# Expert stage: gathering the tokens of four experts at once, token pieces stationary and 256 pick columns moving, no turning of tokens

## The chip, the cores and the metric

One Trainium2 chip, one of its cores. The metric is the device time of one launch in microseconds (us); the median of three runs of the kernel before is 2372.9 us (2370.32 to 2373.47).

## The reference, cut to what matters

The reference is two transformer blocks on 512 tokens of width 1024. The change touches only the last part of the second block, a mixture of 32 experts. Each token is routed to two experts of one group; an expert is a gated feed-forward of width 256:

```
y[e] = (silu(h @ w_gate[e]) * (h @ w_up[e])) @ w_down[e]     # [1024x256], [1024x256], [256x1024]
x    = x + gt2 * sum over the token's two experts of weight * y[e]
out  = rms_norm(x) * g_final
```

The kernel computes an expert only for tokens that picked it: at most 64 of them (64 "slots") in a round. With these inputs one round is enough, so that the stage is 16 pairs of experts, each run once. All is float32; the weights of a pair are six tensors of 1 MB.

## The kernel before, in words

**What runs where.** The expert stage is written out by hand for five engines, which meet at semaphores. SyncE (line 630, helper `expert_load`) issues six loads of 1 MB for each pair of experts: two gate, two up, two down. All but pair 1 use the same six buffers `EXPERT_W`; pair 1 has six of its own (`SECOND_W`). The weights of pairs 0 and 1 are loaded ahead, while the router still works. A load into a buffer waits until the matmuls that read it are done: the gate loads of the next pair wait for the first half of `gu_done`, the up loads for the second, the down loads for `down_made`. Pairs 2, 3, 4 and so on are thus each loaded while the pair ahead of them is computed, part by part.

**One pair on TensorE** (`expert_pair`). (1) Gate and up, line 1366: for each of the two parts and each of the 8 pieces of the model width, one float32 matmul for each expert of the pair, with 64 columns of tokens stationary and 256 weight columns moving; the two experts use different halves of the array. 64 records in the trace. (2) Two `gather` calls for the *next* pair, line 1339: `PICKS` (a 0/1 matrix that says which token goes to which slot, 128 tokens x 128 slots, one for each of four blocks of tokens) is stationary, 512 columns of the tokens' features are moving; each value is the sum of a low and a high part in the rounded format fp32r, hence 2 x 4 matmuls in each call, 16 for a pair. The result has slots on the partitions. (3) Two transposes of the hidden values (line 1374). (4) `turn_tokens`, line 1349: the gathered tokens, copied by ScalarE from PSUM to `TOK` (line 1884), are turned by eight transposes, so that features lie on the partitions; ScalarE copies them to `XE` (line 1888), which has two halves, one for each pair in turn. (5) Down, line 1387: 16 matmuls, 64 columns stationary and 512 moving.

**The other engines.** VectorE makes `PICKS` for a pair in two operations (`place`, line 2624), after the down product of the pair ahead; it multiplies silu(gate) with up (line 2664), copies the turned hidden values (line 2666) and half of the result (line 2669). ScalarE takes the silu (line 1900) and copies the other half of the result (line 1908), and issues the store of the 64 + 64 rows (512 KB) to a scratch tensor in HBM, line 1911. When all pairs are stored, GpSimd fetches each token's two rows (line 1989), VectorE mixes them, TensorE turns them back (line 1401), and the last norm follows.

**Ahead of the stage.** Router, softmax and ranks on VectorE; then ScalarE rounds the tokens to `H2_HIGH`, and VectorE makes `H2_LOW` (`low_tokens`, line 2600) in two halves of four operations. The first half comes before the ranks, the second after the first two `place`. The first gathering starts with `PICKS` and the first half of `H2_LOW`.

**Loops.** On TensorE pairs 0 and 1 are written out; the others run in a loop of 7 turns with two pairs each (line 1393).

Of the kernel before, what the change touches and what calls it, by code (L numbers as in the profile page):

```python
# [32 lines left out]
SLOTS = 64  # L33
# [121 lines left out]
def build(nc, a, stop=99):  # L155

    with ExitStack() as ctx:
        offset_of = {}
# [5 lines left out]
        def sem(name):  # L164
            return ctx.enter_context(nc.semaphore(name))
# [136 lines left out]
        H2_LOW = rounded("h2_low", offset_of["arena"] + 4096 * 4, 4, D)  # L302
        PICKS = rounded("picks", offset_of["arena"] + 10240 * 4, 2, 4, 2 * SLOTS)
        TOK = area(36864, 2, 512)
        TOK_BANK = (7, 0)
        XE = area(8192, 2, 8, 2 * SLOTS)
        SG, MH, MHT = area(11264, 256), area(11520, 256), area(11776, 2, 2 * SLOTS)
# [10 lines left out]

        RK, RM = area(15520, 4, 32), area(15648, 4, 34)
        NRD, SINK = area(15844, 4), area(15848, 12)  # L320
# [62 lines left out]
        h2_high, h2_low = sem("h2_high_made"), sem("h2_low_made")  # L383
        tok_copied, tok_turned = sem("tokens_copied"), sem("tokens_turned")
        logits_copied, logits_turned = sem("logits_copied"), sem("logits_turned")
# [282 lines left out]
        def _(pe):  # L668
# [126 lines left out]
            for q in range(4):  # L795
# [14 lines left out]
                for s in range(2):  # L810
                    j = 2 * q + s
# [521 lines left out]

            def gather(value, par, hf):

                pe.wait_ge(placed, value)
                for tt in range(4):
                    for i_, x_ in enumerate((H2_LOW, H2_HIGH)):
                        mm = pe.matmul(ps[:, hf, :], PICKS[:, par, tt, :], x_[:, tt, hf * 512:hf * 512 + 512],  # L1339
                                       start=(tt == 0 and i_ == 0), stop=(tt == 3 and i_ == 1))  # L1340
                mm.then_inc(gathered, 1)

            tok_rows = TOK.rearrange("s h c -> s (h c)").rearrange("s (p k) -> s k p", k=KT)

            def turn_tokens(value, hf):

                pe.wait_ge(tok_copied, value)
                for k in range(4):
                    mm = pe.transpose(ps[:, TOK_BANK[hf], k * P:k * P + P], tok_rows[:, hf * 4 + k, :], ident)
                mm.then_inc(tok_turned, 1)  # L1350
# [7 lines left out]
            def expert_pair(pair, j, weights, full_, loaded):  # L1358
                pe.wait_ge(xe_ready, pair * 2 + 2)
                for part in range(2):  # L1360
                    for k in range(KT):
                        for e in range(2):
                            if k == 0:
                                pe.wait_ge(full_[2 * part + e], loaded)
                            w = weights[2 * part + e].rearrange("p (k c) -> p k c", c=256)
                            mm = pe.matmul(ps[e * SLOTS:(e + 1) * SLOTS, 2 + part, 0:256],  # L1366
                                           XE[:, j, k, e * SLOTS:(e + 1) * SLOTS], w[:, k, :],
                                           start=(k == 0), stop=(k == KT - 1))
# [22 lines left out]
            expert_pair(0, 0, EXPERT_W, expert_full, 16)  # L1391
            expert_pair(1, 1, SECOND_W, second_full, 16)
            with pe.Fori(1, rounds * 8) as q:
                for j in range(2):

                    expert_pair(q * 2 + j, j, EXPERT_W, expert_full, q * 32 + j * 16)

            for tt in range(4):
# [10 lines left out]
        def _(act):  # L1409
# [471 lines left out]

            def copy_tokens(value, hf):
                act.wait_ge(gathered, value)
                act.activation(TOK[:, hf, :], ps[:, hf, :], ACT.Copy).then_inc(tok_copied, 1)

            def tokens(value, par, hf):
                act.wait_ge(tok_turned, value)
                act.activation(XE[:, par, 4 * hf:4 * hf + 4].rearrange("p k s -> p (k s)"), ps[:, TOK_BANK[hf], :],
                               ACT.Copy).then_inc(xe_ready, 1)

            copy_tokens(1, 0)
            copy_tokens(2, 1)
            tokens(1, 0, 0)
            tokens(2, 0, 1)
            with act.Fori(0, rounds) as r:
                with act.Fori(0, 8) as i:
                    for j in range(2):
                        pair = r * 16 + i * 2 + j
# [8 lines left out]
                        act.wait_ge(y_stored[j], r * 128 + i * 16 + 16)  # L1907
# [3 lines left out]
                        act.dma_start(ybuf[:, bass.ds(i * 2 + j, 1), :].rearrange("t e d -> t (e d)"),  # L1911
                                      YO[:, j, :]).then_inc(y_stored[j], 16)
                for tt in range(4):
                    act.wait_ge(mixed[tt], r + 1)
# [80 lines left out]
        def _(dve):  # L1995
# [619 lines left out]
            lk.done(ts(RM[:, :, 0:32], RM[:, :, 0:32], far, None, ALU.add))  # L2615
            lk.done(ts(RM[:, :, 32:34], RM[:, :, 0:2], -float(SLOTS), None, ALU.add))
# [4 lines left out]
            def place(col_, par, second):  # L2621

                rank_ = RM[:, :, col_:col_ + 1] if isinstance(col_, int) else RM[:, :, bass.ds(col_, 1)]
                tt(PICKS[:, par, :, second * SLOTS:(second + 1) * SLOTS], SLOT_NO.unsqueeze(1).broadcast_to([P, 4, SLOTS]),
                   rank_.broadcast_to([P, 4, SLOTS]), ALU.is_equal).then_inc(placed, 1)

            place(0, 0, 0)
            place(1, 0, 1)
            low_tokens(1)

# [16 lines left out]
            with dve.Fori(0, rounds) as r:  # L2647
# [22 lines left out]

                dve.wait_ge(placed, r * 32 + 34)
                ts(RM, RM, -float(SLOTS), None, ALU.add).then_inc(round_link, 1)
# [70 lines left out]
```

## Time and profile before

| what | value |
|---|---|
| median of three runs | 2372.9 us |
| the profiled execution, its own time | 2371.32 us |
| its span in the trace | 2369.5 us |
| mean granted TensorE clock | 0.967 |
| TensorE busy | 2126.9 us (90% of the span) |
| VectorE, ScalarE, GpSimd busy | 1117.7, 713.0, 220.8 us |
| moved by DMA | 292.99 MB, mean 124 GB/s |

The span is cut by the work before and after the first and last instruction, hence the 1.8 us between it and the execution's own time. The share of 90% is a mean over stages with different limits. The expert stage runs from about 2051 us to 2327 us of the span; the end of the kernel (results fetched, mixed, normed, stored) from there on.

### The profile page before, as it was taken

To read this page: it belongs to the slowest core of one execution; us is meant where nothing else is said; L and a number is where in the kernel's file an instruction comes from. 1 tells how busy PE (TensorE), PEld (TensorE's weight loads), DVE (VectorE), ACT (ScalarE), POOL (GpSimd) and SP (SyncE) were. 2 spreads that over 40 slices of the span, in tenths; PEclk is the share of its full clock that TensorE was granted. 3 is DMA by queue.
4 is the path that set the end of the run, shared out by engine and by line. 5 is a ranking of instruction groups with operands and counts; after the bars stand their busy time and mean duration, and the time that the engine had idled before them with its cause. 6 is when DMAs were issued, how large, how long until landed. Compare 5 with 4: busy or idle time off the path is not lost.

```text
span 2369.5 us, 41679 instructions
## 1 busy us (share of the span) xinstructions
PE 2126.9 (90%) x17962; PEld 1483.2 (63%) x17962; DVE 1117.7 (47%) x2005; ACT 713.0 (30%) x1093; POOL 220.8 (9%) x104
## 2 busy tenths in 40 slices
PE   7968787878989999988989999989899999799994
PEld 5364646464436889765668888868555687456652
DVE  4444444443756555345567774263455633511113
ACT  2322222221231222354343332252244622422221
POOL 0020202020000000000123443420000000000001
PEclk9999899999989999999999999999999999799998
DMA  8201010102547566100423332244120232579994
GB/s 259 83 10 54 4 47 11 47 12 86 158 154 235 172 193 187 54 1 27 134 71 89 101 94 84 94 103 104 34 80 17 64 97 94 226 286 401 403 408 170
DMA packets 215532, 292.99 MB, mean 124 GB/s; under 512 B 7304, under 2 KB 191536, under 8 KB 207184
## 3 DMA queue, kind: packets, MB, share of 16 engines
q1 hardware_dynamic: 210784, 274.85, 34.6%
q0 software_dynamic: 2288, 7.44, 1.5%
q10 hardware_dynamic: 2304, 8.39, 0.9%
q8 instruction: 126, 2.06, 0.4%
q14 instruction: 30, 0.25, 0.0%
HBM read 279.84 MB, written 10.81 MB: 123 GB/s over the span
## 4 chain that ended last, share of the span: by engine, by line
PE 78%; DVE 8%; DMA 5%; ACT 4%; issue 4%; SPq 1%; POOL 0%; POOLq 0%; DVEq 0%; ACTq 0%
PE ps L682 12%; PE ps L1154 10%; PE ps L995 8%; PE ps L783 6%; PE ps L963 6%; PE ps L1185 5%; PE ps L1366 4%; DMA ring<-in_w_up 3%; PE ps L1019 3%; PE ps L1213 3%; PE ps L1049 2%; PE ps L876 2%; PE ps L1065 2%; PE ps L1136 2%; PE ps L1339 2%
## 5 line engine op out<-in xcount | busy, mean ns | idle before, releaser
L682 PE MATMUL ps<-hT,ring 128*128 128x512 f32 (+1 forms) x480 | 212.7, 599 | 3.1 <-ACT hT L1439 2.4
L783 PE MATMUL ps<-arena 64*64 64x64 f32 x6144 | 137.7, 231 | 52.4 <-issue 30.1
L1942 POOL TENSOR_TENSOR w_low<-ring,w_high 128x2048 fp32r<-128x2048 f32 x22 | 101.8, 4626 | 820.4 <-ACT w_high L1683 820.4
L682 PEld LDWEIGHTS ps<-hT,ring 128*128 128x128 f32 (+1 forms) x480 | 89.8, 189 | 120.3 <-issue 117.6
L783 PEld LDWEIGHTS ps<-arena 64*64 64x64 f32 x6144 | 121.6, 142 | 66.6 <-issue 57.5
L1154 PE MATMUL ps<-h_high,w_low 128*128 128x512 f32 x352 | 140.2, 398 | 6.6 <-DVE h_low L2381 6.5
L1154 PE MATMUL ps<-h_high,w_high 128*128 128x512 f32 x352 | 140.3, 399 | 0.0
L1154 PE MATMUL ps<-h_low,w_high 128*128 128x512 f32 x352 | 138.8, 394 | 0.0
L2268 DVE CUSTOM_DVE_ANT_0 arena<-ps,arena 128x256 f32<-128x256 f32 (+3 forms) x160 | 66.9, 468 | 124.4 <-PE ps L1065 124.3
L1469 ACT ACTIVATE arena<-ps 128x512 f32<-128x512 f32 x104 | 61.3, 597 | 193.2 <-PE ps L783 193.2
L1366 PE MATMUL ps<-ring,arena 128*64 128x256 f32 x960 | 111.3, 380 | 4.2 <-DMA ring<-in_w_up 3.3
L2403 DVE TENSOR_TENSOR rstd<-arena 128x512 f32<-128x512 f32 x22 | 98.5, 4478 | 17.5 <-ACT arena L1725 17.5
L995 PE MATMUL ps<-h_high,w_low 128*128 128x512 f32 x256 | 102.6, 401 | 2.6 <-issue 2.6
L682 PE MATMUL ps<-arena,ring 128*128 128x512 f32 (+1 forms) x208 | 95.2, 613 | 8.3 <-DVE arena L2489 5.1
L1366 PEld LDWEIGHTS ps<-ring,arena 128*64 128x64 f32 x960 | 74.8, 137 | 44.1 <-issue 7.7
L995 PE MATMUL ps<-h_low,w_high 128*128 128x512 f32 x256 | 102.1, 399 | 0.0
L995 PE MATMUL ps<-h_high,w_high 128*128 128x512 f32 x256 | 101.8, 398 | 0.0
L1625 ACT ACTIVATE arena<-arena,small 128x384 f32<-128x384 f32 (+6 forms) x96 | 68.0, 708 | 111.0 <-DVE small L2276 111.0
L783 PE MATMUL ps<-const,arena 64*64 64x64 f32 x2304 | 60.1, 243 | 37.0 <-DVE arena L2144 20.3
L1935 POOL TENSOR_TENSOR arena<-arena,const 128x512 f32<-128x512 f32 x40 | 49.9, 1270 | 460.4 <-PE ps L783 460.4
L2018 DVE SCALAR_TENSOR_TENSOR arena<-arena,small 128x256 f32<-128x256 f32 x168 | 81.4, 484 | 14.8 <-DMA arena<-in_w_ada 9.1
L1720 ACT ACTIVATE arena<-ps,cols 128x512 f32<-128x512 f32 x44 | 34.2, 778 | 159.1 <-PE ps L1154 159.1
(423 smaller groups left out, 4404.5 us busy)
## 6 DMA issues: line engine op xcount, KB each, us to landing
ring<-in_w_in SPq DMA_DIRECT2D x54, 1024.0 KB, 5.3
arena<-in_w_ada SPq DMA_DIRECT2D x80, 512.0 KB, 4.0
arena<-in_w_down SPq DMA_DIRECT2D x32, 1024.0 KB, 9.2
ring<-in_w_gate SPq DMA_DIRECT2D x30, 1024.0 KB, 9.9
ring<-in_w_up SPq DMA_DIRECT2D x30, 1024.0 KB, 11.1
ring<-in_w_up SPq DMA_DIRECT2D x44, 512.0 KB, 4.7
ring<-in_w_down SPq DMA_DIRECT2D x8, 1024.0 KB, 5.1
y_scratch<-arena ACTq DMA_DIRECT2D x16, 512.0 KB, 8.0
```

The costliest lines, as they stand in the source:

```text
L682: mm = pe.matmul(dst, w[:, k, hf * P:hf * P + width], rhs(k), start=(start and k == 0), stop=(stop and k == kts - 1))
L783: mm = pe.matmul(ps[o, bank + s, c % 4 * C:c % 4 * C + C], tmp[s][l][r, cc], eye64[r] if x is eye64 else tmp[s][x][r, cc], start=(i == 0), ...
L963: mm = pe.matmul(ps[:, bank, :], w_[:, k, hf * P:hf * P + P], x_, start=(k == 0 and i_ == 0), stop=(k == n_ - 1 and i_ == 2))
L995: mm = pe.matmul(ps[:, bank, :], w_[:, k, hf * P:hf * P + P], x_[:, k, :], start=(k == 0 and i_ == 0), stop=(k == KT - 1 and i_ == 2))
L1019: mm = pe.matmul(ps[:, hh % 4, tt * 256:tt * 256 + 256], x_[:, k, tok:tok + P], w_[:, k, :], start=(k == 0 and i_ == 0), stop=(k == KT - 1 ...
L1154: mm = pe.matmul(ps[:, (2 * (m - first) + g) % 4, :], w_[:, k, :], x_[:, k, :], start=(k == 0 and i_ == 0), stop=(k == KT - 1 and i_ == 2))
L1185: mm = pe.matmul(ps[:, hh % 4, :], w_[:, k, hf * P:hf * P + P], x_, start=(kt == 0 and i_ == 0), stop=(kt == FT - 1 and i_ == 2))
L1213: mm = pe.matmul(ps[:, o % 4, :], w_[:, k, hf * P:hf * P + P], x_[:, k, :], start=(k == 0 and i_ == 0), stop=(k == KT - 1 and i_ == 2))
L1366: mm = pe.matmul(ps[e * SLOTS:(e + 1) * SLOTS, 2 + part, 0:256], XE[:, j, k, e * SLOTS:(e + 1) * SLOTS], w[:, k, :], start=(k == 0), stop= ...
L1942: pool.tensor_tensor(W_LOW[:, slot_, :], ring[:, slot_, :], W_HIGH[:, j % 2, :].bitcast(F32), ALU.subtract).then_inc(w_low, 1)
L2018: ins = stt(ACC[:, j % 5, :], w[:, k, :], c[k], ACC[:, j % 5, :], ALU.mult, ALU.add)
L2403: tt(val, sil[:, jj % 2, :], cvt[jj % 2][1], ALU.mult).then_inc(dve_link, 1)
```

## The change

`PICKS` holds the picks of four experts (two pairs, a "step"): 256 slots for each block of 128 tokens. `gather(k)` makes the k-th of the 8 feature pieces for all four experts: a piece of the tokens, 128 tokens x 128 features (every eighth feature, a stride of 8 elements), is stationary, and the 256 picks move. The result has the features on its partitions already, so `turn_tokens`, `TOK` and ScalarE's copies into it are gone. Eight gathers of eight matmuls each make one step's tokens. They lie in two PSUM banks, two pieces in a bank; ScalarE copies a bank (a "quarter", 512 columns) to `XE[par][quarter]`, in turn for even and odd steps. In the first pair of a step (j = 0) TensorE does gathers 0 and 1 before the hidden transposes and 2 and 3 behind them; in the second pair (j = 1) gather 4 before, 5 behind, and 6 and 7 after the down product. Before the first pair all eight are done, after all of `H2_LOW` and four `place`. VectorE makes all four `place` of the next step at the start of the first pair of a step, once the gathers that read the picks are done. TensorE's loop has three turns of four pairs; steps 0 and 1 are written out. Loads and stores are the same, except that ScalarE's loop has four turns of four pairs.

```diff
-        PICKS = rounded("picks", offset_of["arena"] + 10240 * 4, 2, 4, 2 * SLOTS)
-        TOK = area(36864, 2, 512)
-        XE = area(8192, 2, 8, 2 * SLOTS)
+        PICKS = rounded("picks", offset_of["arena"] + 10240 * 4, 4, 4 * SLOTS)
+        XE = [[area(at, 2, 4 * SLOTS) for at in (8192, 8704, 9216, 9728)], [area(at, 2, 4 * SLOTS) for at in (36864, 37376, 15872, 32768)]]
...
-            def gather(value, par, hf):
-                pe.wait_ge(placed, value)
+            def gather(k):
                 for tt in range(4):
                     for i_, x_ in enumerate((H2_LOW, H2_HIGH)):
-                        mm = pe.matmul(ps[:, hf, :], PICKS[:, par, tt, :], x_[:, tt, hf * 512:hf * 512 + 512],
+                        rows = x_[:, tt, :].rearrange("s (p k) -> s k p", k=KT)
+                        mm = pe.matmul(ps[:, k // 2 % 2, k % 2 * 256:k % 2 * 256 + 256], rows[:, k, :], PICKS[:, tt, :],
                                        start=(tt == 0 and i_ == 0), stop=(tt == 3 and i_ == 1))
-            for hf in range(2):
-                pe.wait_ge(h2_low, 4 * hf + 4)
-                gather(2, 0, hf)
-            for hf in range(2):
-                turn_tokens(2, hf)
+            pe.wait_ge(h2_low, 8)
+            pe.wait_ge(placed, 4)
+            for k in range(KT):
+                if k in (4, 6):
+                    pe.wait_ge(xe_ready, k // 2 - 1)
+                gather(k)
...
+            def expert_pair(step, j, par, pair, weights, full_, loaded):
+                if j == 0:
+                    pe.wait_ge(xe_ready, step * 4 + 3)
                 for part in range(2):
                     for k in range(KT):
+                        if j == 0 and part == 0 and k == 6:
+                            pe.wait_ge(xe_ready, step * 4 + 4)
...
-                gather(pair * 2 + 4, 1 - j, 0)
-                gather(pair * 2 + 4, 1 - j, 1)
+                if j == 0:
+                    pe.wait_ge(placed, step * 4 + 8)
+                    gather(0)
+                    gather(1)
+                else:
+                    pe.wait_ge(xe_ready, step * 4 + 5)
+                    gather(4)
...
-                turn_tokens(pair * 2 + 4, 0)
-                turn_tokens(pair * 2 + 4, 1)
+                if j == 0:
+                    gather(2)
+                    gather(3)
+                else:
+                    gather(5)
...
                 mm.then_inc(down_made, 1)
+                if j:
+                    pe.wait_ge(xe_ready, step * 4 + 6)
+                    gather(6)
+                    gather(7)
...
-                        copy_tokens(pair * 2 + 3, 0)
-                        copy_tokens(pair * 2 + 4, 1)
-                        tokens(pair * 2 + 3, 1 - j, 0)
-                        tokens(pair * 2 + 4, 1 - j, 1)
+                        tokens(quarters + 2 * j, 1 - par, 2 * j)
+                        if j == 0:
+                            tokens(quarters + 1, 1 - par, 1)
...
+                        if j:
+                            tokens(quarters + 3, 1 - par, 3)
...
-            place(0, 0, 0)
-            place(1, 0, 1)
+            for which in range(4):
+                place(which, which)
             low_tokens(1)
...
-                        dve.wait_ge(down_made, pair + 1)
-                        for second in range(2):
-                            place(i * 4 + (2 * j + 2 + second), 1 - j, second)
+                        if j == 0:
+                            dve.wait_ge(gathered, r * 32 + i * 4 + 4)
+                            for which in range(4):
+                                place(i * 4 + (4 + which), which)
```

## Rows read from the trace of the kernel before

**Rows 1.** Windows of the expert stage: length, busy us of each engine, clock, DMA share, GB/s
```profile
2110.00:2140.00 30.00, 27.76 (x184) 17.44 (x180) 3.15 (x7) 7.21 (x12) 0.00 (x0) 1.00 1.01 409
2260.00:2290.00 30.00, 28.94 (x194) 18.43 (x192) 3.73 (x9) 7.21 (x12) 0.00 (x0) 1.00 1.01 404
```

**Rows 2.** DMA of 2120 to 2320 us: GB/s in 40 slices of 5 us, packets, queues
```profile
GB/s 428 400 429 424 317 349 435 424 396 428 424 365 392 428 415 416 429 423 280 428 421 398 397 430 422 388 428 429 351 428 428 399 398 422 415 342 428 434 392 279
DMA packets 14973, 80.32 MB, mean 402 GB/s; under 512 B 1329, under 2 KB 1329, under 8 KB 9009
q1 hardware_dynamic: 13245, 74.03, 92.1%
q10 hardware_dynamic: 1728, 6.29, 7.7%
```

**Rows 3.** Timeline of SyncE's queue: start, us, the load issued (two of them)
```profile
2107.69 0.89 SPq L630 DMA_DIRECT2D arena<-in_w_down  x2
2111.38 0.98 SPq L630 DMA_DIRECT2D ring<-in_w_gate  x2
...
2296.51 0.96 SPq L630 DMA_DIRECT2D ring<-in_w_gate  x2
```

**Rows 4.** Waits between 2107 and 2320 us: us in total, times, longest
```profile
PEld ps L1366 <- DMA ring<-in_w_up: 6.5, 7, 1.8
```

**Rows 5.** One window of 4 us just before pair 3 starts
```profile
2104.00:2108.00 4.00, 4.00 (x23) 1.57 (x24) 0.12 (x1) 0.89 (x3) 0.00 (x0) 1.00 0.60 254
```

**Rows 6.** Timeline of pair 2, PE and DVE: start, us, instructions, idle before and releaser
```profile
2091.26 7.08 PE L1366 MATMUL ps<-ring,arena 128*64 128x256 f32 x64
...
2098.39 0.42 DVE L2664 TENSOR_TENSOR arena<-ps,arena 128x256 f32<-128x256 f32 x1 [5.43 <-PE ps L1366]
...
2102.06 0.38 PE L1374 MATMUL ps<-const,arena 128*128 128x128 f32 x2
2102.47 0.42 DVE L2666 COPY arena<-ps 128x256 f32<-128x256 f32 x1 [3.66 <-PE ps L1374]
...
2102.91 1.16 PE L1349 MATMUL ps<-const,arena 128*128 128x128 f32 x8 [0.47 <-ACT arena L1884]
...
2103.99 3.65 PE L1387 MATMUL ps<-arena 128*64 128x512 f32 x16
...
2107.48 4.70 PE L1366 MATMUL ps<-ring,arena 128*64 128x256 f32 x42
```

**Rows 7.** Window of 12 us of line 1019 alone: PE busy, PEld busy, clock
```profile
888.00:900.00 12.00, 11.80 (x99) 11.62 (x99) 1.00 0.44 143
```

**Rows 8.** Timeline of PEld: eight weight loads with stride 8 (L1349), without (L1401)
```profile
2102.90 0.97 PEld L1349 LDWEIGHTS ps<-const,arena 128*128 128x128 f32 x8 [0.71 <-ACT arena L1884]
...
2350.13 0.86 PEld L1401 LDWEIGHTS ps<-const,arena 128*128 128x128 f32 x8 [0.34 <-DVE arena L2643]
```

**Rows 9.** Timeline of the stage's start, PE and DVE
```profile
2050.01 0.75 DVE L2624 TENSOR_TENSOR picks<-arena 128x256 fp32r<-128x256 f32 x2
2050.68 2.49 DVE L2600 TENSOR_TENSOR h_low<-arena,h_high 128x512 fp32r<-128x512 f32 x4
2050.90 0.77 PE L1339 MATMUL ps<-h_low,picks 128*128 128x512 f32 x1 [3.51 <-DVE picks L2624]
...
2058.77 3.46 PE L1366 MATMUL ps<-ring,arena 128*64 128x256 f32 x30 [0.72 <-ACT arena L1888]
```

**Rows 10.** Windows around the first gathering
```profile
2050.90:2053.90 3.00, 3.00 (x7) 2.42 (x8) 2.93 (x7) 0.00 (x0) 0.00 (x0) 0.50 0.02 5
```

**Rows 11.** Timeline of the last pair, PE and DVE
```profile
2313.86 3.67 PE L1366 MATMUL ps<-ring,arena 128*64 128x256 f32 x30 [0.69 <-DMA ring<-in_w_up]
2317.57 0.43 DVE L2664 TENSOR_TENSOR arena<-ps,arena 128x256 f32<-128x256 f32 x1 [6.69 <-PE ps L1366]
...
2326.88 0.69 DVE L2669 COPY arena<-ps 128x512 f32<-128x512 f32 x1 [4.80 <-PE ps L1387]
```

**Rows 12.** Window of 4 us in the last pair
```profile
2316.00:2320.00 4.00, 4.00 (x25) 2.81 (x21) 0.43 (x1) 0.39 (x1) 0.00 (x0) 1.00 0.60 244
```

**Rows 13.** DMA of 2060 to 2120 us: the queue of instruction fetches
```profile
q8 instruction: 3, 0.05, 0.3%
```

More of the change, by code:

```diff
@@ L1332, in _ @@
             rounds = pe.value_load(NRD[0:1, 0:1].bitcast(I32), min_val=1, max_val=T // SLOTS)
-            def gather(value, par, hf):
-                pe.wait_ge(placed, value)
+            def gather(k):
                 for tt in range(4):
                     for i_, x_ in enumerate((H2_LOW, H2_HIGH)):
-                        mm = pe.matmul(ps[:, hf, :], PICKS[:, par, tt, :], x_[:, tt, hf * 512:hf * 512 + 512],
+                        rows = x_[:, tt, :].rearrange("s (p k) -> s k p", k=KT)
+                        mm = pe.matmul(ps[:, k // 2 % 2, k % 2 * 256:k % 2 * 256 + 256], rows[:, k, :], PICKS[:, tt, :],
                                        start=(tt == 0 and i_ == 0), stop=(tt == 3 and i_ == 1))
[L1341 to L1350, printed above, removed]
-            for hf in range(2):
-                pe.wait_ge(h2_low, 4 * hf + 4)
-                gather(2, 0, hf)
-            for hf in range(2):
-                turn_tokens(2, hf)
-            def expert_pair(pair, j, weights, full_, loaded):
-                pe.wait_ge(xe_ready, pair * 2 + 2)
+                if k % 2:
+                    mm.then_inc(gathered, 1)
+            pe.wait_ge(h2_low, 8)
[7 more added lines that the diff above has]
+                    pe.wait_ge(xe_ready, step * 4 + 3)
                 for part in range(2):
                     for k in range(KT):
+                        if j == 0 and part == 0 and k == 6:
+                            pe.wait_ge(xe_ready, step * 4 + 4)
                         for e in range(2):
@@ L1389, in expert_pair @@
                 mm.then_inc(down_made, 1)
[L1391 to L1396, printed above, removed]
+                if j:
+                    pe.wait_ge(xe_ready, step * 4 + 6)
+                    gather(6)
+                    gather(7)
+            expert_pair(0, 0, 0, 0, EXPERT_W, expert_full, 16)
+            expert_pair(0, 1, 0, 1, SECOND_W, second_full, 16)
+            for j in range(2):
+                expert_pair(1, j, 1, 2 + j, EXPERT_W, expert_full, 32 + 16 * j)
+            with pe.Fori(1, rounds * 4) as q:
+                for par in range(2):
+                    for j in range(2):
+                        expert_pair(q * 2 + par, j, par, q * 4 + (2 * par + j), EXPERT_W, expert_full, q * 64 + (32 * par + 16 * j))
+            pe.wait_ge(xe_ready, rounds * 32 + 4)
             for tt in range(4):
@@ L1880, in _, with tokens @@
             ybuf = a["y_scratch"].rearrange("(e t) d -> t e d", t=2 * SLOTS)
-            def copy_tokens(value, hf):
+            def tokens(value, par, quarter):
                 act.wait_ge(gathered, value)
[L1884 to L1894, printed above, removed]
+                act.activation(XE[par][quarter].rearrange("p k s -> p (k s)"), ps[:, quarter % 2, :], ACT.Copy).then_inc(xe_ready, 1)
+            for quarter in range(4):
+                tokens(quarter + 1, 0, quarter)
             with act.Fori(0, rounds) as r:
-                with act.Fori(0, 8) as i:
-                    for j in range(2):
-                        pair = r * 16 + i * 2 + j
+                with act.Fori(0, 4) as i:
+                    for par, j in ((0, 0), (0, 1), (1, 0), (1, 1)):
+                        pair = r * 16 + i * 4 + (2 * par + j)
+                        quarters = r * 32 + i * 8 + (4 * par + 5)
                         act.wait_ge(gu_done, pair * 2 + 3)
                         act.activation(SG, ps[:, 2, 0:256], ACT.Silu).then_inc(silu_m, 1)
-                        copy_tokens(pair * 2 + 3, 0)
-                        copy_tokens(pair * 2 + 4, 1)
-                        tokens(pair * 2 + 3, 1 - j, 0)
-                        tokens(pair * 2 + 4, 1 - j, 1)
+                        tokens(quarters + 2 * j, 1 - par, 2 * j)
+                        if j == 0:
+                            tokens(quarters + 1, 1 - par, 1)
                         act.wait_ge(down_made, pair + 2)
-                        act.wait_ge(y_stored[j], r * 128 + i * 16 + 16)
+                        act.wait_ge(y_stored[j], r * 128 + i * 32 + (16 * par + 16))
                         act.activation(YO[:, j, 0:512], ps[:, 4, :], ACT.Copy).then_inc(copied["A"], 1)
@@ L2619, in _, with place @@
             ts(SINK[:, 8:9], ZERO, 1.0, None, ALU.add).then_inc(gu_done, 2)
-            def place(col_, par, second):
+            def place(col_, which):
                 rank_ = RM[:, :, col_:col_ + 1] if isinstance(col_, int) else RM[:, :, bass.ds(col_, 1)]
-                tt(PICKS[:, par, :, second * SLOTS:(second + 1) * SLOTS], SLOT_NO.unsqueeze(1).broadcast_to([P, 4, SLOTS]),
+                tt(PICKS[:, :, which * SLOTS:(which + 1) * SLOTS], SLOT_NO.unsqueeze(1).broadcast_to([P, 4, SLOTS]),
                    rank_.broadcast_to([P, 4, SLOTS]), ALU.is_equal).then_inc(placed, 1)
-            place(0, 0, 0)
-            place(1, 0, 1)
+            for which in range(4):
+                place(which, which)
             low_tokens(1)
```

12 lines of the change are left out of this document (5 added, 7 removed).

## The prediction

> **What bounds the kernel now.** Only the expert stage is touched, so I read that stage alone: first windows of 30 us over it. Between 2110 and 2290 us both limits seem reached: TensorE is busy 28 to 29 of 30 us at full clock, and the DMA share is 1.01 [rows 1]. Which of the two ends last? The DMA view of 2120 to 2320 us gives 402 GB/s over 200 us, with slices of 5 us at 428 whenever only weights flow, and dips to 280 to 400 where a result store (queue 10) runs beside them [rows 2]. The issues of the gate loads are a clock for the pairs: from the issue in pair 3 to that in pair 14 there are 2296.51 - 2111.38 = 185.1 us for 11 pairs, 16.83 us each [rows 3]. A pair moves six weights and one store, 6.5 x 1.0486 = 6.82 MB, and 6.82 / 16.83 us = 405 GB/s, which is what the windows show at share 1.01. TensorE alone needs less: pair 2, whose weights were there early, took from 2091.26 to 2107.48, 16.22 us [rows 6]. The 0.6 us between are the waits for up weights, 6.5 us in 7 of the pairs [rows 4]. So from pair 3 on the stage goes by the DMA engines, with TensorE 0.6 us a pair behind them. Before pair 3 it goes by TensorE: the DMA engines still have holes there, such as share 0.60 at 2104 to 2108 [rows 5]. From the down loads of pair 3, issued at 2107.69 [rows 3], the DMA engines have work until the last down weights, near 2318.4: in the window 2316 to 2320 the share is 0.60 [rows 12]. Behind that comes the last pair's rest on TensorE alone.
>
> **The change, part by part.** *Price of one gather matmul.* 128x128 stationary, 256 columns moving, fp32r: this form stands in the trace at line 1019, 99 of them in 11.80 us, 0.119 us each, their weight loads included [rows 7]. The stationary piece now has a stride of 8 elements. The turned tokens are read so too: eight loads in 0.97 us against 0.86 without a stride [rows 8], 0.014 us more each. Beside matmuls of 0.107 us of columns (256 at 2.4 GHz) that may be hidden or not, so bounds are 0.119 and 0.133; I take 0.119, because the strided loads (0.97 / 8 = 0.121) go hardly slower than the matmuls themselves.
> A rule of the Trainium skill speaks against the change: "TensorE: Matmul & The Clock Gate", The mechanism, has weight loads overlap matmuls in flight only where they use other row groups. By it a gather matmul would be a load and a matmul one after the other; line 1019 disagrees, since 0.119 us has no room for both, so the rule is only a rival here: by the rule the sum would be near that of rival B, slower by some 30 us, by the row it is the sum below.
>
> *One pair on TensorE.* From the end of gate and up (2098.39) to the start of down (2103.99) there are 5.60 us [rows 6]: gathering 3.67, hidden transposes, the wait of 0.47 for ScalarE's copy, eight turns. Of these the hidden transposes stay, about 0.4. In their place: 32 gather matmuls a pair (64 a step), 3.8 us. So a pair takes 16.22 - 5.60 + 0.4 + 3.8 = 14.8 and saves 1.4 us; with the strided price of 0.133 it saves 0.95, with no gap at all between matmuls (0.107) 1.8. The waits that could take this back: the hidden product on VectorE needs 0.42 us and a gather of 8 takes 0.95; the copy of the turned hidden values ends at 2102.89, 0.83 us after the transposes started [rows 6], and gather 5 alone covers it narrowly. The last quarter of tokens is copied about 2.7 us after down (two gathers 1.9, one copy 0.6, signals), 0.8 us into the next gate part, while the wait stands before piece 6, some 2.7 us into it. VectorE's four `place` (0.37 each [rows 9], 1.5 us) run behind the last gather, under 7.1 us of gate and up. ScalarE loses two copies a pair. All of that costs nothing while gate and up last 7.1 us; no load or store is added or moved.
>
> *The start.* Two more `place` push the second half of the low tokens by 0.75 us, and TensorE now waits for all of it: before, it started at 2050.90; now at 2050.68 + 0.75 + 2.49 + signals = 2054.0 [rows 9]. It does 64 matmuls where it did 16 and 8. In the first 3.0 us the granted clock is 0.50 (1.2 GHz), after an idle stretch [rows 10]; the new idle stretch is 3 us longer, so I let the first 3.3 us again be at half the speed: 15 matmuls at 0.22, then 49 at 0.119 = 5.8. Gate of pair 0 starts at 2054.0 + 3.3 + 5.8 = 2063.1 against 2058.77 [rows 9]: 4.4 us late. Bounds: 2.8 if the clock is full at once, 6 with strided loads and a longer slow stretch.
>
> *To the saturated stretch.* Pairs 0, 1 and 2 give back 3 x 1.4 = 4.2 us. So the down loads of pair 3 are issued 0.2 us later than at 2107.69.
>
> *In it.* Same bytes, same order of issues, TensorE with more slack (2.0 us a pair instead of 0.6): 0, bounds -1.5 and +1.5 us for a rate that differs by 0.1 us a pair. The saved 1.4 us a pair turn into longer waits at line 1366 for up weights.
>
> *The end.* In the last pair the up weights arrive at 2313.86, and VectorE sees down finished at 2326.88; from up's end at 2317.57 that is 9.31 us [rows 11]. Now it is gather 4 (0.95), transposes 0.4, gather 5 (0.95), down 3.65 = 5.95, since gathers 6 and 7 come behind: 3.4 us less. The down weights are there at 2318.4, needed at 2319.9, a cover of 1.5 us. Gathers 6 and 7 lie under the store and the fetch of the results.
>
> *Sum.* +4.4 - 4.2 + 0 - 3.4 = -3.2 us. The profiled execution took 2371.32 us, 1.6 below the median of 2372.9; against the median the forecast is 2369.7 us.
>
> **The rivals.** *A, the DMA rate rises.* With loads asked for earlier, the dips at the stores [rows 2] might fill. At 428 GB/s throughout, a pair would take 15.9 us, above TensorE's 14.8: 0.9 x 12 pairs = 11 us more, 2358.7. For it: the slices at 428. Against it: the dips come with the stores, which stay, and the queue is never empty now at share 1.01 [rows 1]. Chance 0.13, mostly of a part of it.
> *B, weight loads exposed (slower).* Place: line 1339's successor, each gather matmul. Its price would be 0.121 (a strided load) + 0.107 = 0.23 us, and it decides the stage from the price at which TensorE reaches 16.83 us: 11.0 + 32 x p, p = 0.18. At 0.23 a pair takes 18.4 us: 1.6 us more than now over 15 pairs, 24, and 64 x 0.11 = 7 more at the start, less 2 at the end: 29 + 4 = 33 us, 2406. Line 1019 speaks against it [rows 7], though not with a stride. Chance 0.05.
> *C, TensorE's longer loop.* A pair has some 114 matmul and as many weight load records; the loop grows from two pairs to four. Up to 2120 us there are 3 instruction fetches [rows 13], and from 2120 to 2320 us queue 8 has no row at all [rows 2]: the loop of two pairs is held by the engine. If one of four is not, each of three turns fetches 4 blocks of 16 KB through full DMA engines; at some 9 us before the first is there, less 2 us of slack, 3 x 7 = 21 us, 2391. Chance 0.05.
> The Trainium skill, "Runtime: NRT & Kernel Launch", Instruction fetch mechanics, says that a taken branch out of the held window must fetch before it goes on, and gives TensorE 2048 instructions; by that figure the loop of some 950 would be held, and the sum stays as it is. No run here shows the figure.
> *D, the change does less than it says at the start or in the last pair* (a late copy, a late down load): the 3.4 us of the end or the 4.2 of three pairs lost, about +1, 2374. Chance 0.12.
>
> **How the numbers follow.** Forecast as summed 0.65, A 0.13, B 0.05, C 0.05, D 0.12. A measurement of this kernel can tell 0.2% from no change, 4.7 us, so the limits are 2368.2 and 2377.6. The forecast's own spread (start -1.6 to +1.6, rate 1.5, price of the gather +1.5, run to run 1.5) is about 2366 to 2373, a third of it under 2368.2: faster 0.65 x 0.35 + 0.12 = 0.35; slower B, C and a little of D = 0.13; same 0.52. The range takes in the own spread, half of A and D: 2362 to 2375.5.
>
> **What would show it.** Right: line 1349 gone; gather matmuls at 0.12 us; gate of pair 0 starting near 2063; pairs of 16.8 us and DMA share 1.0 from pair 3 on; waits of TensorE for weights up from 6.5 to some 23 us; 6 us between the end of up and of down in the last pair. Wrong: pairs of under 16.6 us with more than 410 GB/s (A), gather pitch over 0.18 (B), queue 8 active beyond 2130 us with gaps at every fourth pair (C).

## The result, and the profile after

| | before | after |
|---|---|---|
| median | 2371.61 us (2368.29 to 2373.47, 4 runs) | 2413.43 us (2411.8 to 2415.94, 4 runs) |
| ratio | | 1.0183, 95% interval 1.0171 to 1.0196 |
| the profiled execution, its span | 2371.32, 2369.5 us | 2413.67, 2411.9 us |

The change makes the kernel 42 us slower, where 3 us faster was forecast. The gather matmuls tell it at once. First the source view of their line (duration ns min/median/max), then a few rows of their timeline, after the change:

```profile
L1336 PEld LDWEIGHTS ps<-picks,h_low x288: 312/337/345, 2055.6 to 2371.7; 128*128 128x128 f32 x144
L1336 PE MATMUL ps<-picks,h_low x288: 398/403/607, 2055.6 to 2371.9; 128*128 128x256 f32 x144
```
```profile
2210.49 0.40 PE L1336 MATMUL ps<-picks,h_low 128*128 128x256 f32 x1
2210.60 0.34 PEld L1336 LDWEIGHTS ps<-picks,h_high 128*128 128x128 f32 x1
2210.73 0.41 PE L1336 MATMUL ps<-picks,h_high 128*128 128x256 f32 x1
...
2213.60 0.40 PE L1336 MATMUL ps<-picks,h_low 128*128 128x256 f32 x1
2213.70 0.34 PEld L1336 LDWEIGHTS ps<-picks,h_high 128*128 128x128 f32 x1
2213.84 0.41 PE L1336 MATMUL ps<-picks,h_high 128*128 128x256 f32 x1
```

They start 0.24 us apart (2213.60 to 2213.84; 0.241 on average over a long row of them) where 0.119 was taken, and their weight loads last 0.337 us instead of the 0.189 of line 1019. The stage as a whole, in one window (length, PE, PEld, DVE, ACT, POOL busy, clock, DMA share, GB/s), answers [rows 1]:

```profile
2112.00:2352.00 240.00, 240.00 (x1450) 175.45 (x1448) 27.93 (x62) 31.52 (x54) 0.00 (x0) 1.00 0.89 359
```

TensorE is busy all of the 240 us, the DMA share has fallen from 1.01 to 0.89 and the rate from about 405 to 359 GB/s. In the list of waits no row of TensorE waiting for weights is left. The issues of the gate loads [rows 3] and the last pair [rows 11] after the change:

```profile
2131.48 1.03 SPq L627 DMA_DIRECT2D ring<-in_w_gate  x2
...
2338.64 0.88 SPq L627 DMA_DIRECT2D ring<-in_w_gate  x2
...
2353.54 7.08 PE L1359 MATMUL ps<-ring,arena 128*64 128x256 f32 x64
...
2360.66 0.42 DVE L2669 TENSOR_TENSOR arena<-ps,arena 128x256 f32<-128x256 f32 x1 [6.03 <-PE ps L1359]
...
2368.51 0.69 DVE L2674 COPY arena<-ps 128x512 f32<-128x512 f32 x1 [5.09 <-PE ps L1388]
```

Pairs 3 to 14 take (2338.64 - 2131.48) / 11 = 18.83 us each instead of 16.83, and 11.0 + 32 x 0.241 = 18.7 is rival B's formula with the measured price. And the start, which answers [rows 9]:

```profile
2051.68 1.42 DVE L2628 TENSOR_TENSOR picks<-arena 128x256 fp32r<-128x256 f32 x4
2053.02 2.49 DVE L2604 TENSOR_TENSOR h_low<-arena,h_high 128x512 fp32r<-128x512 f32 x4
...
2055.56 0.61 PE L1336 MATMUL ps<-picks,h_low 128*128 128x256 f32 x1 [6.41 <-DVE h_low L2604]
...
2071.16 7.13 PE L1359 MATMUL ps<-ring,arena 128*64 128x256 f32 x64
```

Counted from the first `place` (2050.01 before, 2051.68 after), so that what came ahead of the stage drops out, the 42.4 us of span divide so:

| stretch | before | after | difference |
|---|---|---|---|
| first `place` to gate of pair 0 | 8.8 | 19.5 | +10.7 |
| gate of pair 0 to gate of pair 15 | 250.3 | 282.4 | +32.0 |
| gate of pair 15 to VectorE's last copy | 17.8 | 15.0 | -2.8 |

The other 2.4 us lie ahead of the stage (1.7) and behind it; nothing there was changed. Of the kernels below, two had one execution each in a slower state (6692.43 and 3081.98 us), which their ratios leave out.

### The profile page after: what moved, and what is told of

Its sections match the earlier page's. It is cut to its first block, busy times and chain, and to the rows that moved or that the text cites. A ratio compares the mean times of both kernels' runs of the same rounds, so it can differ in the third digit from the quotient of the medians.

```text
span 2411.9 us, 41980 instructions
## 1 busy us (share of the span) xinstructions
PE 2182.8 (91%) x18130; PEld 1553.9 (64%) x18130; DVE 1118.6 (46%) x2007; ACT 690.4 (29%) x1057; POOL 220.8 (9%) x104
## 4 chain that ended last, share of the span: by engine, by line
PE 81%; DVE 8%; ACT 4%; issue 4%; DMA 2%; SPq 1%; POOL 0%; POOLq 0%; DVEq 0%; ACTq 0%
PE ps L679 11%; PE ps L1151 10%; PE ps L992 8%; PE ps L780 6%; PE ps L1336 6%; PE ps L960 6%; PE ps L1182 5%; PE ps L1359 5%; PE ps L1210 3%; PE ps L1016 3%; PE ps L1388 2%; PE ps L1046 2%; PE ps L873 2%; PE ps L1062 2%; PE ps L1133 2%
## 5 line engine op out<-in xcount | busy, mean ns | idle before, releaser
L1336 PE MATMUL ps<-picks,h_low 128*128 128x256 f32 x288 | 120.7, 419 | 6.4 <-DVE h_low L2604 6.4
L1336 PE MATMUL ps<-picks,h_high 128*128 128x256 f32 x288 | 116.9, 406 | 0.0
L1336 PEld LDWEIGHTS ps<-picks,h_low 128*128 128x128 f32 x288 | 96.6, 335 | 19.2 <-issue 12.6
L1336 PEld LDWEIGHTS ps<-picks,h_high 128*128 128x128 f32 x288 | 97.7, 339 | 0.0
```

Source lines behind the costliest of these rows:

```text
L1336: mm = pe.matmul(ps[:, k // 2 % 2, k % 2 * 256:k % 2 * 256 + 256], rows[:, k, :], PICKS[:, tt, :], start=(tt == 0 and i_ == 0), stop=(tt = ...
```

## The experiments

In each expectation theory S, R and so on are told anew. The kernel before was timed again beside the experiments, and "before" is the median beside the kernel in question: 2371.87 us for pieces side by side, the strides, TensorE with little to do and piece order; 2369.35 us for the next four; 2371.5 us (one execution) for the transposes at the end. The kernels with four kinds of gather were made for the prices of single instructions, and each was executed only once.

### Pieces side by side

```diff
-                        rows = x_[:, tt, :].rearrange("s (p k) -> s k p", k=KT)
+                        rows = x_[:, tt, :].rearrange("s (k p) -> s k p", k=KT)
```

> The changed kernel with one edit: a stationary piece is 128 features side by side instead of every eighth, so the tokens reach the experts in another order of features (this part of the computation is changed). Theory S (the stride makes the weight load slow, and that alone made the change slow): the gather matmuls go at 0.119 us each instead of 0.24, as at line 1019, pairs from pair 3 on at 16.8 us by the DMA engines, and the kernel takes what was forecast for the change, 3 us less than before, 2368 to 2369. Theory R (a 128x128 fp32r weight load is exposed behind only 256 moving columns in this place, whatever its stride): 0.24 us each still, and 42 us more than before.

Measured: 2361.86 us, ratio 0.9959 (0.9941 to 0.9977): 10 us less than before, 52 less than the change. The same source view, and the window of its saturated stretch:

```profile
L1336 PEld LDWEIGHTS ps<-picks,h_low x288: 186/192/330, 2054.1 to 2320.0; 128*128 128x128 f32 x144
L1336 PE MATMUL ps<-picks,h_low x288: 278/283/583, 2054.1 to 2320.1; 128*128 128x256 f32 x144
```
```profile
2112.00:2304.00 192.00, 182.17 (x1334) 117.52 (x1332) 26.37 (x59) 29.11 (x50) 0.00 (x0) 1.00 1.02 416
```

Only the stride was taken away, and the loads fall back to 0.19 us: theory S holds, R falls. But the kernel is 7 us better than S foresaw. By the stretches of the table above: start 13.2 (+4.5 to before; forecast +4.4), gate of pair 0 to gate of pair 15 240.6 (-9.7; forecast -4.2), end 14.3 (-3.4; forecast -3.4). The one term that is off is the saturated stretch: 16.35 us a pair and 416 GB/s instead of 16.83 and 405. In the two pairs ahead of that stretch, where only TensorE counts, a pair takes 14.9 us (forecast 14.8).

### Which stride costs

Gathers 0 and 1 read pieces side by side, 2 and 3 with stride 2, 4 and 5 with stride 4, 6 and 7 with stride 8:

```diff
-                        rows = x_[:, tt, :].rearrange("s (p k) -> s k p", k=KT)
-                        mm = pe.matmul(..., rows[:, k, :], PICKS[:, tt, :],
+                        if k < 2:
+                            mm = pe.matmul(..., x_[:, tt, k * P:k * P + P], PICKS[:, tt, :],
+                        elif k < 4:
+                            mm = pe.matmul(..., x_[:, tt, 0:256].rearrange("s (p k) -> s k p", k=2)[:, k % 2, :], PICKS[:, tt, :],
...
```

> One look for prices only (features reach the experts in another order): gathers 0 and 1 with pieces side by side, 2 and 3 with stride 2, 4 and 5 with stride 4, 6 and 7 with stride 8, each on a line of its own. Theory S: 0.119 us a matmul at stride 1 and 0.24 at stride 8; between them, if the load reads a fixed number of neighbouring bytes at a time, the price rises in steps, some 0.12, 0.12 to 0.15, 0.15 to 0.24. Theory R: 0.24 on all four lines.

Measured: 2375.63 us in the one execution. The source views of the four lines (stride 1, 2, 4, 8), and the timeline where the second gives way to the third:

```profile
L1336 PEld LDWEIGHTS ps<-picks,h_high x72: 187/189/338, 2051.4 to 2309.5; 128*128 128x128 f32 x72
L1339 PEld LDWEIGHTS ps<-picks,h_high x72: 193/196/199, 2054.7 to 2311.6; 128*128 128x128 f32 x72
L1342 PEld LDWEIGHTS ps<-picks,h_high x72: 329/330/334, 2056.7 to 2326.4; 128*128 128x128 f32 x72
L1345 PEld LDWEIGHTS ps<-picks,h_high x72: 336/338/341, 2060.5 to 2334.0; 128*128 128x128 f32 x72
```
```profile
2056.41 0.28 PE L1339 MATMUL ps<-picks,h_low 128*128 128x256 f32 x1
2056.53 0.28 PE L1339 MATMUL ps<-picks,h_high 128*128 128x256 f32 x1
...
2057.11 0.40 PE L1342 MATMUL ps<-picks,h_low 128*128 128x256 f32 x1
2057.35 0.40 PE L1342 MATMUL ps<-picks,h_high 128*128 128x256 f32 x1
```

Stride 2 goes at 0.120 us a matmul, stride 4 at 0.233, stride 8 at 0.241: nearly all of the price comes in one step, between 8 and 16 bytes. The Trainium skill states this step ("SBUF — State Buffer", the note on cachelines): SBUF is read in lines of 16 bytes, and full speed needs at least two hits in a line. Two float32 at stride 2 share such a line, two at stride 4 don't, and the runs agree with it on where the step lies. The same note counts four float32 as the distance that can be strided for free; taken as a stride of 4, the 0.233 us measured here speak against it. The prediction did not weigh this rule.

The same kernel shows a second thing. Between 2112 and 2312 us:

```profile
2112.00:2312.00 200.00, 199.51 (x1360) 141.93 (x1355) 27.07 (x60) 29.39 (x50) 0.00 (x0) 1.00 1.00 401
```

TensorE works 199.5 of 200 us and in all of the stage waits once, for 0.5 us, for weights. By the prices it needs 11.0 + 5.7 = 16.7 us a pair, and pairs take 16.9 on average, so it is the bound, and yet the DMA share is 1.00. A share of 1.0 is therefore no proof that the DMA engines are the bound.

### TensorE with little to do

Only the last of the four blocks of tokens is multiplied:

```diff
+                        if tt == 3:
-                        mm = pe.matmul(..., start=(tt == 0 and i_ == 0), stop=(tt == 3 and i_ == 1))
+                            mm = pe.matmul(..., start=(i_ == 0), stop=(i_ == 1))
```

> The changed kernel with only two of the eight matmuls of each gather (the last of the four blocks of tokens; the other three are left out of the sum), strided as in the change. It asks whether the DMA engines really hold the stage once TensorE is fast: TensorE needs 11.0 + 8 x 0.24 = 12.9 us a pair. If the DMA engines hold it at 16.83 us a pair from pair 3 on, as the prediction has it: pairs 16.8 us, waits for weights of some 3.9 us a pair, saturation from 9 us earlier than before, 4 us less at the end, in all about 13 us less than before. If loads asked for earlier run faster (rival A): pairs under 16.4 us and 20 us or more less than before.

Measured: 2353.2 us, ratio 0.9931 (0.9912 to 0.9949), 16 to 19 us less than before, between the two cases and nearer to the second. TensorE is busy 135 of 160 us:

```profile
2130.00:2290.00 160.00, 135.19 (x874) 83.29 (x872) 22.57 (x50) 24.32 (x42) 0.00 (x0) 1.00 1.02 419
```

The last ten gate loads are 16.34 us apart on average. TensorE has time to spare and asks for each part early, so this is the wall of the DMA engines: 419 GB/s, some 16.3 us a pair, and not the 16.83 that the kernel before shows. Pairs under 16.4 us are what the second case said; its 20 us in all were not reached.

### The saved 1.4 us a pair given back

Three low products of each gather are done twice, in the kernel with pieces side by side:

```diff
-                    for i_, x_ in enumerate((H2_LOW, H2_HIGH)):
+                    for i_, x_ in enumerate((H2_LOW,) * (1 if tt == 0 else 2) + (H2_HIGH,)):
```

> The kernel with contiguous pieces (e1_contiguous), with three of the low products of each gather done twice (three parts are counted twice in the sum), 11 matmuls instead of 8: TensorE needs 12 x 0.119 = 1.4 us more a pair, 16.2 us as before the change. Theory T (pairs went from 16.83 to 16.35 us because TensorE asks for the loads earlier): the pairs go back to 16.7 to 16.9 us, the rate to some 405 GB/s, and the kernel takes 2371 to 2374 us, 6 to 8 us of the 10 gained given back or more. Theory U (the rate rose for another reason, such as where the stores and picks lie now): pairs stay at 16.35 to 16.45 us, and only the first three pairs, the start and the last pair give back 4 x 1.4 + 2.9 = 8 us less what hides; rate stays over 414 GB/s.

Measured: 2384.31 us, ratio 1.005 (1.0034 to 1.0066), in 200 us:

```profile
2110.00:2310.00 200.00, 193.43 (x1453) 131.27 (x1453) 26.64 (x59) 29.60 (x50) 0.00 (x0) 0.99 0.98 390
```

Pairs take 17.36 us on average. The direction is theory T's: TensorE alone now needs 16.35 us a pair (the first two), the rate falls from 416 to 390 GB/s, and the pairs go well above both this need and the wall. The size was missed by 10 us. One pair of 20.7 us is 4 of it: TensorE waited 2.53 us for down weights, the granted clock fell, and the mean clock over that pair was 0.92. The other ten pairs take 17.0 us, or 400 GB/s, near the 16.83 and 405 of the kernel before. TensorE also waits 6.6 us for down weights, which the kernel before did not do. That a busier TensorE takes the rate away directly is ruled out by the kernel with piece order and two sets below: there it is busy 197.6 of 200 us at 418 GB/s. So this run shows that, with one set of buffers, TensorE's slack sets the rate; its own 390 is not that of the kernel before.

### Two sets of weight buffers in the kernel before

```diff
-            with sp.Fori(2, rounds * 8) as q:
+            with sp.Fori(1, rounds * 8) as q:
-                for j in range(2):
+                for j, (buffers, signals) in enumerate(((EXPERT_W, expert_full), (SECOND_W, second_full))):
                     pair = q * 2 + j
+                    if j:
+                        sp.wait_ge(results_free, (q // 8) + 1)
                     for part, w, c_ in PARTS:
-                        sp.wait_ge(*((gu_done, pair * 2 + 1), (gu_done, pair * 2 + 2), (down_made, pair + 1))[part])
+                        sp.wait_ge(*((gu_done, pair * 2 - 1), (gu_done, pair * 2), (down_made, pair))[part])
```

> The kernel before the change with the two sets of weight buffers and nothing else. TensorE needs 16.22 us a pair; if the DMA engines can do a pair in 16.3, TensorE waits for hardly any weights (under 2 us), all 16 pairs go at 16.2 us, and the kernel takes 8 us less than before, 2362 to 2365. If 16.83 us a pair was the wall of the DMA engines, they still have a head start of 50 us of work and the same 2362 to 2365 follows, but with waits for weights in the last pairs and a rate near 405 GB/s there.

Measured: 2361.38 us, ratio 0.9958 (0.9943 to 0.9973). This is 8 us less than before, as expected. No row of a wait for weights is left, and twelve gate issues (2100.06 to 2278.34) are 16.21 us apart, TensorE's own time; the time in all would be the same by both cases of the expectation, so it is the waits and the rate that tell them apart. One window:

```profile
2080.00:2280.00 200.00, 194.38 (x1326) 121.54 (x1324) 28.40 (x63) 47.80 (x80) 0.00 (x0) 1.00 1.01 413
```

With the first 5 us slice left out (221 GB/s, the stretch just begins) the other 39 slices are between 396 and 433 GB/s, on average 418: the dips to 280 to 350 of [rows 2] are gone, though the same stores run. They were not the price of the stores, as the prediction had it, but came with the single set: a part's load could be asked for only when TensorE had read that part. That for a moment nothing is ready to be moved while the share still counts 1.0 is my reading of it; no run shows that moment by itself.

### Piece order without a stride

The kernel that computes the reference. ScalarE writes the tokens in piece order when it copies them out of PSUM, and the first half of the low tokens then suffices for the first four gathers:

```diff
-                act.activation(H2T[:, g // 2, g % 2 * 512:g % 2 * 512 + 512], ps[:, 4 + g % 2, :], ACT.Copy).then_inc(h2_ready, 1)
+                act.activation(H2T[:, g // 2, :].rearrange("s (k p) -> s k p", k=KT)[:, :, g % 2 * 64:g % 2 * 64 + 64],
+                               ps[:, 4 + g % 2, :].rearrange("s (p k) -> s k p", k=KT), ACT.Copy).then_inc(h2_ready, 1)
...
-            pe.wait_ge(h2_low, 8)
+            pe.wait_ge(h2_low, 4)
             pe.wait_ge(placed, 4)
             for k in range(KT):
+                if k == 4:
+                    pe.wait_ge(h2_low, 8)
```

> As the first, but computing all of the reference: ScalarE's copy out of PSUM writes the tokens in piece order (stride 128 elements in its output), so that pieces lie side by side, and the first four gathers wait only for the first half of the low tokens. Theory S: 0.119 us a gather matmul; gate of pair 0 starts some 2 us later than before instead of 4.4; in all 5 to 6 us less than before, if ScalarE's eight copies stay at 0.6 us. Theory R: 0.24 us a gather matmul, some 40 us more than before.

Measured: 2364.75 us, ratio 0.9969 (0.9957 to 0.9981). Theory S again, and 7 us less than before, where 5 to 6 were expected. ScalarE's copies stay at 0.60 us with the reordered read and write. The start is 11.9 us, 3.1 more than before instead of 2: the first gathers run for 5.7 us at the clock of 0.5, where 3.3 had been taken. In the profiled execution a second thing appears: after TensorE waited 2.04 us for up weights, the granted clock dropped.

```profile
2123.46 5.35 PE L1361 MATMUL ps<-ring,arena 128*64 128x256 f32 x30 [2.04 <-DMA ring<-in_w_up]
```
```profile
2122.00:2125.00 3.00, 1.54 (x12) 0.97 (x14) 0.00 (x0) 0.00 (x0) 0.00 (x0) 0.88 1.02 416
2125.00:2128.00 3.00, 3.00 (x18) 1.72 (x16) 0.00 (x0) 0.00 (x0) 0.00 (x0) 0.55 1.04 422
```

The up half that takes 3.67 us at full clock took 5.35, and that pair 19.2 us.

### Piece order and two sets of weight buffers

Both edits together; the last quarter of the odd steps' tokens moves to another place, since the down weights of the second set now stay where it was.

> The kernel in piece order (e2_piece_order), and in addition two sets of weight buffers for all pairs (even pairs one, odd pairs the other), so that each load may be issued a pair earlier; all of the reference is computed. If the DMA engines' wall is some 418 GB/s, 16.3 us a pair, and not the 16.8 of before: they run from pair 0's gate on without a hole, last down weights about 228 us later, TensorE needs 14.8 us a pair; the stage ends some 25 us earlier than before, 2343 to 2350 us. If 405 GB/s is the wall, 16.8 us a pair, 7 us later than that, 2350 to 2357.

Measured: 2347.89 us, ratio 0.9899 (0.9883 to 0.9914): 21.5 us faster than before and 65 faster than the change, the best kernel of this study, with all of the reference computed, and inside the expected 2343 to 2350 us of the wall of 418 GB/s. Both engines are at their wall:

```profile
2080.00:2280.00 200.00, 197.56 (x1500) 129.76 (x1497) 30.05 (x67) 32.16 (x55) 0.00 (x0) 1.00 1.02 418
```

The rate is 418 GB/s over 200 us without a slice under 397, and TensorE waits for weights only in the last pairs. Pairs go at TensorE's 14.9 us until the DMA engines' head start is used up (the first eleven), and the last three whose length can be read take 16.1, 16.4 and 16.1 us.

### Why the turns gave no warning

The turns read tokens with stride 8 as well, and the trace showed loads of 0.19 us for them. First four kinds of gather: float32 with stride 8, float32 side by side, fp32r with stride 8, fp32r side by side. The edit is the choice of operands, `x_[...].bitcast(F32)` and `PICKS[:, tt, :].bitcast(F32)`, for gathers 0 to 3.

> One look for prices only (features reach the experts in another order; gathers 0 to 3 are full float32 products). The changed kernel with four kinds of gather, each on its own line: 0 and 1 float32 with stride 8, 2 and 3 float32 side by side, 4 and 5 fp32r with stride 8, 6 and 7 fp32r side by side. It asks why the turns of tokens, float32 weight loads with stride 8, gave no warning. Theory F (the stride costs only fp32r): float32 goes at the same time with and without stride, weight loads of about 0.19 us in both. Theory G (the stride costs every weight load about 0.24 us, and a turn hides it in some way of its own): float32 loads with stride 8 take 0.33 us too, and a float32 matmul, whose columns take four times as long, hides them.

The one execution took 2460.34 us. The source views of the first three kinds:

```profile
L1336 PEld LDWEIGHTS ps<-picks,h_high x144: 336/337/340, 2055.0 to 2388.9; 128*128 128x128 f32 x144
L1339 PEld LDWEIGHTS ps<-picks,h_high x144: 190/190/190, 2063.8 to 2396.1; 128*128 128x128 f32 x144
L1342 PEld LDWEIGHTS ps<-picks,h_high x72: 336/337/339, 2070.5 to 2410.9; 128*128 128x128 f32 x72
```

The loads with stride 8 last 0.337 us in float32 too: theory F falls. Then transposes against plain matmuls:

```diff
+                        if k < 2:
+                            mm = pe.transpose(dst, wide, ident)
+                        elif k < 4:
+                            mm = pe.transpose(dst, near, ident)
+                        elif k < 6:
+                            mm = pe.matmul(dst, wide, ident, start=True, stop=True)
+                        else:
+                            mm = pe.matmul(dst, ident, wide, start=True, stop=True)
```

> One look for prices only: the gathers are replaced by products with the 128x128 identity, eight each, each kind on its own line, all float32 (no tokens are gathered: the experts get other numbers). Gathers 0 and 1: transposes of a piece with stride 8; 2 and 3: transposes of a piece side by side; 4 and 5: plain matmuls with the stride-8 piece stationary and the identity moving; 6 and 7: plain matmuls with the identity stationary and the stride-8 piece moving. It asks why the turns of tokens before the change, with stride 8, took weight loads of only 0.19 us. Theory M (in a transpose the weight load is that of the data and is fast for another reason): transposes with stride 8 show loads of 0.19 us, the plain matmul with the same stationary piece 0.337. Theory N (in a transpose the data move and the identity is what is loaded, so that the rows of before never showed a strided weight load): transposes behave like the fourth kind, loads of 0.19 us for both, and only the third kind shows 0.337. The fourth kind also tells what a moving operand with stride 8 costs.

The one execution took 2432.33 us. The source views of the four kinds:

```profile
L1339 PEld LDWEIGHTS ps<-const,h_high x72: 194/196/226, 2048.1 to 2362.4; 128*128 128x128 f32 x72
L1341 PEld LDWEIGHTS ps<-const,h_high x72: 139/141/144, 2051.4 to 2364.4; 128*128 128x128 f32 x72
L1343 PEld LDWEIGHTS ps<-const,h_high x144: 334/334/338, 2053.5 to 2382.7; 128*128 128x128 f32 x144
L1345 PEld LDWEIGHTS ps<-h_high,const x144: 208/208/209, 2061.0 to 2393.8; 128*128 128x128 f32 x144
```

Same piece, same stride, same type: 0.196 us in a transpose, 0.334 in a plain matmul. Side by side a transpose's load is 0.141 and a plain one 0.189 to 0.190. So a transpose's load does feel the stride, by 0.055 us in its record, but in the time from one to the next hardly any of it shows: transposes start 0.113 us apart with the stride and 0.11 without. Theory M is right in what it says of the two durations. N would have strided transposes behave like the fourth kind; they don't, for the fourth kind's matmuls start 0.23 us apart, with loads of 0.208 us. The names in the rows, moving operand first, also put the tokens on the stationary side of a transpose (`ps<-const,h_high`). What makes a transpose's load cheaper stays open.

The fourth kind answers one more question. With the strided piece moving, 128 float32 columns take 0.23 us, where 256 of them side by side took 0.215 (first kernel of this section, line 1339). By this estimate the stride doubles the price of a moving operand too, so with the piece as the moving operand the stride would have had its price as well.

## Why the prediction was wrong, point by point

*The price of a gather matmul* is the step that failed, in the sentence "I take 0.119, because the strided loads (0.97 / 8 = 0.121) go hardly slower than the matmuls themselves". Line 1019 [rows 7] was the right row for the form and says nothing of a stride; the only strided loads in the trace [rows 8] are those of transposes, and they were read as if they were a plain matmul's. Measured: 0.241 us. Even the upper bound, 0.133, came from there, so the range did not hold the result. Rival B had nearly the right price for the wrong reason: it added a transpose's strided load and the columns, 0.121 + 0.107. The load is exposed not because loads cannot run beside matmuls (side by side they do, at 0.119), but because a strided load alone is longer than the 0.107 us of columns that it runs beside. The start of the stage shows which of the two it is. At a granted clock of 0.50 the columns take 0.213 us (pieces side by side), and yet the strided matmuls start 0.24 us apart there too; a load of 0.121 us and the columns one after the other would be 0.33 by estimate.

*Rival B* was priced at 2406 us; the result was 2413. Its formula for a pair holds (18.7 against 18.83 measured), its start (+11) too (+10.7). What it lacked is 0.011 us a matmul, 6 us in all.

*The start, the three early pairs, the end*: with the stride gone these terms stand as written, +4.5 against +4.4, and -3.4 against -3.4. TensorE's start of gathering was forecast for 2054.0 and is 2055.56 less the 1.67 that came ahead of the stage, 2053.9.

*"In it: 0"* failed as well, hidden behind the first error. The kernel before was not at the DMA engines' wall in its saturated stretch. The wall is 418 to 419 GB/s, 16.3 us a pair (three kernels: TensorE with little to do, and the two with two sets of buffers); the 405 GB/s was what a single set of weight buffers gives with a TensorE that needs 16.2 us. The sign that was misread is the share of 1.01 [rows 1]. With 11 pairs at 0.48 us, this is 5.3 of the 7 us by which the kernel with pieces side by side beat its forecast. Rival A had this mechanism ("with loads asked for earlier, the dips at the stores might fill"), with a chance of 0.13, and its sign of more than 410 GB/s came with pieces side by side. Its rate of 428 was too high. What was held against it, that the dips come with the stores and that the queue is never empty at a share of 1.01, is what the runs with two sets refute.

*Waits, copies, picks, TensorE's loop*: as forecast they cost nothing that shows, for TensorE is busy all of 240 us. Queue 8 has five fetches in 240 us after the change, and no gap follows any turn of the loop, so rival C falls.

## What to carry to other kernels

When a change turns a moving operand into a stationary one, look at the stride of its free dimension first: with 16 bytes or more between float32 elements a 128-column weight load took 0.23 to 0.24 us here and paced the matmuls, whose 256 columns need only 0.107; an engine that copies the data anyway can write it side by side for nothing. A price must come from a row of the same kind of instruction: a transpose's strided load told nothing of a plain matmul's. And a DMA share of 1.0 is not a wall; compare GB/s with the best stretch of the same kind of traffic, and ask what a second buffer would give.

## What the runs showed that I had not expected

The strided load does not go by TensorE's clock. After the change the first gathers run at a clock of 0.50, later ones at 1.00, at the same 0.24 us:

```profile
2056.00:2058.00 2.00, 2.00 (x10) 2.00 (x10) 1.76 (x7) 0.00 (x0) 0.00 (x0) 0.50 0.03 8
2060.00:2062.00 2.00, 2.00 (x10) 2.00 (x9) 2.00 (x1) 0.32 (x1) 0.00 (x0) 1.00 0.00 0
```
```profile
2056.93 0.44 PE L1336 MATMUL ps<-picks,h_high 128*128 128x256 f32 x1
2057.17 0.44 PE L1336 MATMUL ps<-picks,h_low 128*128 128x256 f32 x1
...
2060.48 0.40 PE L1336 MATMUL ps<-picks,h_low 128*128 128x256 f32 x1
2060.72 0.41 PE L1336 MATMUL ps<-picks,h_high 128*128 128x256 f32 x1
```

With pieces side by side the same matmuls need 0.213 us at the low level (1.2 GHz) and 0.12 at the high one (2.4 GHz). And a TensorE that waits for weights was in some cases granted less clock afterwards. In three kernels it fell to the low level behind one wait each: 2.04 us in piece order, 2.04 us with little to do (the down product behind it took 6.64 us instead of 3.65), 2.53 us in the slowed kernel. Waits just as long left it at 1.00: 2.09 us with pieces side by side, 2.26 us with little to do. What decides it, no run here shows. The second of these falls, from the kernel with little to do:

```profile
2104.49 6.64 PE L1389 MATMUL ps<-arena 128*64 128x512 f32 x16 [2.04 <-DMA arena<-in_w_down]
```
